# A two-layer transformer kernel: quads of the first attention turned one ahead, other orders in both output projections, a held weight split, and a helper for the second weight tile

## What is computed

```python
h = rmsnorm(x, attn_pre_g); proj = h @ w_in          # queries, keys, values, gates
o_nsa = nsa_attention(...)   # compressed, selected and window keys, 8 heads in 2 groups
o_swa = swa_attention(...)   # window of 128 keys with sinks, 8 heads in 2 groups
x = x + rmsnorm(concat(o_nsa, o_swa) @ w_o, attn_post_g)
a, u = split(rmsnorm(x, mlp_pre_g) @ w_gate_up); a = causal_dwconv(a)
x = x + rmsnorm((gelu(a) * u) @ w_down, mlp_post_g)
x = x + (p @ w_ple) * sigmoid(x @ w_ple_gate)
# second block: layer 0 differential attention (8 heads, 768 keys), layer 1 grouped queries
h = rms_norm(x, pre_g) * (1 + scale) + shift          # the same for the context
x = x + gate * rms_norm(attention(h @ w_in) @ w_out, post_g)
```

## Time and profile before

| | us |
|---|---|
| median of 3 runs (lowest, highest) | 1668.63 (1667.78, 1669.62) |
| the profiled execution, its own time | 1671.54 |
| its span, first to last instruction | 1670.2 |
| TensorE matmuls busy | 1563.2 |
| VectorE busy | 1059.8 |
| GpSimd busy | 719.2 |
| ScalarE busy | 612.8 |
| mean granted clock of TensorE | 0.976 |

### The profile page before, as it was taken

The page is one execution under the profiler, slowest core; times in us unless marked ns, Lnnn a source line. Parts: engine busy times, 40 slices in busy tenths (PEclk is TensorE's granted clock), DMA queues, the critical chain, the costliest instruction groups (busy, mean ns, idle before and its releaser), DMA issues. The chain is left out here.

```text
span 1670.2 us, 21955 instructions
## 1 busy us (share of the span) xinstructions
PE 1563.2 (94%) x7933; PEld 1294.0 (77%) x7933; DVE 1059.8 (63%) x2146; ACT 612.8 (37%) x1496; POOL 719.2 (43%) x676
## 2 busy tenths in 40 slices
PE   5899799999999999999999999999997989899997
PEld 4786444688877787877798999899985767898886
DVE  7646666457777767748866565665666468656544
ACT  3213656242122220113443544444345255344431
POOL 6856000328678648685544124412444304423330
PEclk9998999999999999999999999999998999999999
DMA  6623000315444436553321011101111411111221
GB/s 181 187 80 91 11 1 1 127 64 150 122 139 133 120 107 215 176 189 115 120 64 39 14 50 51 46 18 39 51 51 51 151 64 51 52 50 39 64 89 51
DMA packets 115884, 142.58 MB, mean 85 GB/s; under 512 B 11048, under 2 KB 75200, under 8 KB 115776
## 3 DMA queue, kind: packets, MB, share of 16 engines
q1 hardware_dynamic: 89968, 91.77, 18.1%
q10 hardware_dynamic: 25808, 49.40, 9.1%
HBM read 132.74 MB, written 8.40 MB: 85 GB/s over the span
## 5 line engine op out<-in xcount | busy, mean ns | idle before, releaser
L470 POOL TENSOR_SCALAR w_hi<-w_raw 128x512 fp32r<-128x512 f32 x316 | 247.2, 782 | 667.4 <-PE ps L485 510.7
L472 POOL TENSOR_TENSOR w_lo<-w_raw,w_hi 128x512 fp32r<-128x512 f32 x316 | 440.3, 1393 | 26.4
L483 PE MATMUL ps<-w_hi,h_hi 128*128 128x384 f32 (+2 forms) x768 | 281.1, 366 | 4.1 <-DVE x L2596 1.8
L484 PE MATMUL ps<-w_lo,h_hi 128*128 128x384 f32 (+2 forms) x768 | 267.5, 348 | 0.0
L485 PE MATMUL ps<-w_hi,h_lo 128*128 128x384 f32 (+2 forms) x768 | 266.9, 348 | 0.0
L483 PE MATMUL ps<-h_hi,w_hi 128*128 128x512 f32 (+1 forms) x616 | 246.4, 400 | 8.0 <-POOL w_lo L472 4.2
L485 PE MATMUL ps<-h_hi,w_lo 128*128 128x512 f32 (+1 forms) x616 | 239.0, 388 | 0.0
L484 PE MATMUL ps<-h_lo,w_hi 128*128 128x512 f32 (+1 forms) x616 | 238.8, 388 | 0.0
L2541 DVE SCALAR_TENSOR_TENSOR mod_acc<-mod_piece,csil,mod_acc 128x512 f32<-128x512 f32 x140 | 158.5, 1171 | 27.0 <-DMA mod_piece<-in_ada_w 22.9
L483 PEld LDWEIGHTS ps<-w_hi,h_hi 128*128 128x128 f32 x768 | 147.0, 191 | 16.0 <-DVE x L2596 2.5
L484 PEld LDWEIGHTS ps<-w_lo,h_hi 128*128 128x128 f32 x768 | 147.2, 192 | 9.7 <-issue 0.5
(11 more groups left out here) (323 smaller groups left out, 2789.3 us busy)
## 6 DMA issues: line engine op xcount, KB each, us to landing
mod_piece<-in_ada_w ACTq DMA_DIRECT2D x96, 256.0 KB, 3.2
w_raw<-in_w_gate_up SPq DMA_DIRECT2D x88, 256.0 KB, 3.2
w_raw<-in_a_w_in SPq DMA_DIRECT2D x128, 128.0 KB, 2.3
w_raw<-in_w_down SPq DMA_DIRECT2D x22, 512.0 KB, 4.0
w_raw<-in_b_w_in SPq DMA_DIRECT2D x20, 512.0 KB, 3.6
w_raw<-in_w_out SPq DMA_DIRECT2D x16, 512.0 KB, 3.8
w_raw<-in_w_in SPq DMA_DIRECT2D x8, 512.0 KB, 4.2
w_raw<-in_w_o SPq DMA_DIRECT2D x8, 512.0 KB, 3.8
```

The costliest lines, as they stand in the source:

```text
L470: pool.tensor_scalar(hi[:, e, :], raw[:, e, :], 1.0, 0.0, ALU.mult, ALU.add).then_inc(*s["pool_step"].up())
L472: m = pool.tensor_tensor(lo[:, e, :], raw[:, e, :], hi[:, e, :], ALU.subtract)
L483: pe.matmul(out, a[0], b[0], start=start, stop=False)
L484: pe.matmul(out, a[0], b[1], start=False, stop=False)
```

## The change

1. `pool_program` no longer makes the high halves of `("kv", 1)`; ScalarE makes them, one copy of 128x1024 for each pair, ahead of its copies of the keys, and GpSimd waits for each copy before its two differences.
2. The split of `("z8", 0)` waits for the query roots (`rms` of `("q8", 0)`) in place of `roped8` of the last key row.
3. `pe_quads` keeps the value product of the last chunk of a quad back until the first turn and the scores of the next quad are issued. `act_quads` makes the exponentials one chunk later, behind that chunk's copy; `dve_quads` scales the next quad ahead of the low halves of the quad before.
4. In the first output projection VectorE scales the rows (`dve_scale_row` serves both projections); its last row is rooted and scaled ahead of the low halves of row 2.
5. In the second output projection y is squared first for every row, the store of a row goes out one row later, row t - 2 is turned after the squares of row t instead of ahead of those of t + 1, and the loads of the tables and VectorE's use of them move one row later.

```diff
+BY_SCALAR = ("kv", 1)
@@ pool_program
                 if tile == ("z8", 0):
-                    pool.wait_ge(*s["roped8"].at(("kv8", TX + 1)))
+                    pool.wait_ge(*s["rms"].at(("q8", 0)))
+            if tile == BY_SCALAR:
+                pool.wait_ge(*s["act_step"].at(("w_hi", q)))
             for e in range(2):
-                pool.tensor_scalar(hi[:, e, :], raw[:, e, :], 1.0, 0.0, ALU.mult, ALU.add).then_inc(*s["pool_step"].up())
-                pool.wait_ge(*s["pool_step"].now())
+                if tile != BY_SCALAR:
+                    pool.tensor_scalar(hi[:, e, :], raw[:, e, :], 1.0, 0.0, ALU.mult, ALU.add).then_inc(*s["pool_step"].up())
+                    pool.wait_ge(*s["pool_step"].now())
@@ act_block_one_attention
+    for q in range(0, KD, 2):
+        pair = (KD + q) // 2
+        act.wait_ge(*s[f"w_loaded{pair % 2}"].at(pair))
+        act.activation(k.place(BY_SCALAR)[0][:, q:q + 2, :], k.w_raw[:, pair % 2, :, :], ACT.Copy, scale=1.0).then_inc(*s["act_step"].up(("w_hi", q)))
@@ pe_quads
+    before = None
     for q in qs:
         ahead = slots_behind(qs, q.n)
-        for i in range(len(q.chunks) + 1):
-            if i < len(q.chunks):
-                pe_quad_turn(k, pe, qs, q, i)
+        for i in range(len(q.chunks)):
+            pe_quad_turn(k, pe, qs, q, i)
             for slot in ahead[2 * i:2 * i + 2]:
                 pe_slot_scores(k, pe, qs, slot)
-            if i > 0:
-                pe_quad_values(k, pe, qs, q, i - 1)
+            if before is not None:
+                pe_quad_values(k, pe, qs, *before)
+            before = q, i
+    pe_quad_values(k, pe, qs, *before)
@@ act_quads
-        ahead = slots_behind(qs, q.n)
-        for i in range(len(q.chunks) + 1):
-            if i < len(q.chunks):
-                act_quad_copy(k, act, qs, q, i)
+        ahead, last = slots_behind(qs, q.n), len(q.chunks) - 1
+        for i in range(last + 1):
+            act_quad_copy(k, act, qs, q, i)
+            for slot in (ahead[2 * i - 2:2 * i] if i > 0 else []):
+                act_slot_exp(k, act, qs, slot)
+            if i == last:
+                for slot in ahead[2 * i:2 * i + 2]:
+                    act_slot_exp(k, act, qs, slot)
             if i == 0 and q.n > 0 and qs[q.n - 1].kind > 0:
                 outputs(qs[q.n - 1])
-            for slot in ahead[2 * i:2 * i + 2]:
-                act_slot_exp(k, act, qs, slot)
@@ dve_quads
+        if q.n + 1 < len(qs):
+            dve_quad_scale(k, dve, qs, qs[q.n + 1])
         if q.n > 0 and qs[q.n - 1].kind > 0:
             outputs(qs[q.n - 1])
-        if q.n + 1 < len(qs):
-            dve_quad_scale(k, dve, qs, qs[q.n + 1])
@@ pe_project_out, turn_out
-        pe.wait_ge(*s["scaled"].at(("out1", t)))
+        pe.wait_ge(*s["dve_step"].at(("out1", t)))
@@ act_project_out
-    act_last_scale(k, act, "y1", TX - 1, k.x2, rows, "out1")
@@ act_add
-    if before and scaled is not None:
-        act.wait_ge(*s["rms"].at((tag, t)))
-        act_scale(k, act, rows(t - 1), x[:, t - 1, :], 2 * t + 1, (scaled, t - 1))
@@ dve_add
-    if tag == "y3" and before:
-        dve_scale_row(k, dve, t - 1)
+    if before:
+        dve_scale_row(k, dve, tag, t - 1)
@@ dve_project_out
+    dve_last(k, dve, "y1", TX - 1)
+    dve.wait_ge(*s["rms"].at(("y1", "x", TX - 1)))
+    dve_scale_row(k, dve, "y1", TX - 1)
     turn_out(TX - 2)
-    dve_last(k, dve, "y1", TX - 1)
     turn_out(TX - 1)
@@ act_out0
     for t in range(TA):
-        if t >= 3:
-            turn_out(t - 3)
-        act_add(..., y_first=t == 1)
-        if t == 2:
-            act.wait_ge(*s["x_out"].at(("7", 1)))
+        act_add(..., y_first=t > 0)
+        if 1 <= t <= TX:
+            act.wait_ge(*s["added"].at(("y3", t - 1)))
+            act.dma_start(k.x_dram[:, t - 1, :], k.x7[:, t - 1, :]).then_inc(*s["x_out"].up(("7", t - 1), 16))
+        if t >= 2:
+            turn_out(t - 2)
+        if t == 3:
+            act.wait_ge(*s["x_out"].at(("7", 2)))
             ...
-        if t < TX:
-            act.wait_ge(*s["added"].at(("y3", t)))
-            act.dma_start(k.x_dram[:, t, :], k.x7[:, t, :]).then_inc(*s["x_out"].up(("7", t), 16))
-    turn_out(TA - 3)
@@ dve_out0
-        if t == TX:
+        if t == TX + 1:
             dve_query_tables(k, dve)
-        dve_add(..., y_first=t == 1)
+        dve_add(..., y_first=t > 0)
```

More of the change, by code:

```diff
@@ L879, in pe_quads @@
         pe_slot_scores(k, pe, qs, slot)
+    before = None
     for q in qs:
         ahead = slots_behind(qs, q.n)
-        for i in range(len(q.chunks) + 1):
-            if i < len(q.chunks):
-                pe_quad_turn(k, pe, qs, q, i)
+        for i in range(len(q.chunks)):
+            pe_quad_turn(k, pe, qs, q, i)
             for slot in ahead[2 * i:2 * i + 2]:
                 pe_slot_scores(k, pe, qs, slot)
-            if i > 0:
-                pe_quad_values(k, pe, qs, q, i - 1)
-        assert 2 * (len(q.chunks) + 1) >= len(ahead)
+            if before is not None:
+                pe_quad_values(k, pe, qs, *before)
+            before = q, i
+        assert 2 * len(q.chunks) >= len(ahead)
+    pe_quad_values(k, pe, qs, *before)
 def pe_mod_sum(k, pe, layer, j, bank, c0=0):
@@ L1531, in act_squares @@
     act.activation(junk[:, :], x, ACT.Square, accum_out=k.halves[:, 0, i:i + 1]).then_inc(*k.sig["sq"].up(event))
-def act_scale(k, act, out, x, i, event):
-    act.activation(out, x, ACT.Copy, scale=k.stat[:, 1, i:i + 1]).then_inc(*k.sig["scaled"].up(event))
 def act_program(k, act):
@@ L1764, in act_project_out @@
             turn_out(t - 2)
-        act_add(k, act, "y1", t, k.x2, k.y2[:, t % 2, :], O_BANKS[t % 2], rows, ("o", t, 1), "out1")
+        act_add(k, act, "y1", t, k.x2, k.y2[:, t % 2, :], O_BANKS[t % 2], rows, ("o", t, 1))
         act.wait_ge(*s["added"].at(("y1", t)))
@@ L1769, in act_project_out, with act_add @@
     turn_out(TX - 2)
-    act_last_scale(k, act, "y1", TX - 1, k.x2, rows, "out1")
     turn_out(TX - 1)
-def act_add(k, act, tag, t, x, yt, banks, rows, prod, scaled, y_first=False):
+def act_add(k, act, tag, t, x, yt, banks, rows, prod, y_first=False):
     s = k.sig
@@ L1803, in act_last_squares @@
     act_squares(k, act, x[:, t, :], rows(t), 2 * t + 3, (tag, "x", t))
-def act_last_scale(k, act, tag, t, x, rows, scaled):
-    act.wait_ge(*k.sig["rms"].at((tag, "x", t)))
-    act_scale(k, act, rows(t), x[:, t, :], 2 * t + 3, (scaled, t))
 def act_gate_up(k, act):
@@ L2138, in act_out0 @@
     for t in range(TA):
-        if t >= 3:
-            turn_out(t - 3)
-        act_add(k, act, "y3", t, k.x7, k.y7[:, t % 2, :], OUT0_BANKS[t % 3], rows, ("out0", t, 1), None, y_first=t == 1)
-        if t == 2:
-            act.wait_ge(*s["x_out"].at(("7", 1)))
+        act_add(k, act, "y3", t, k.x7, k.y7[:, t % 2, :], OUT0_BANKS[t % 3], rows, ("out0", t, 1), y_first=t > 0)
+        if 1 <= t <= TX:
[5 more added lines that the diff above has]
+            act.wait_ge(*s["x_out"].at(("7", 2)))
             act.dma_start(k.cosb[:, :, :], k.ins["cos_b"]).then_inc(*s["tabb_in"].up("all", 16))
@@ L2265, in act_out1 @@
     for t in range(TX):
-        act_add(k, act, "y4", t, k.x9, k.y9[:, t % 2, :], OUT1_BANKS[t], None, ("out1", t, 1), None)
+        act_add(k, act, "y4", t, k.x9, k.y9[:, t % 2, :], OUT1_BANKS[t], None, ("out1", t, 1))
         act.wait_ge(*s["added"].at(("y4", t)))
@@ L2569, in dve_end_copy, with dve_scale_row @@
     dve.tensor_copy(k.end_place(n), k.ps[0:KD, MOD_END_BANKS[n], 0:P]).then_inc(*s["end_copied"].up(n))
-def dve_scale_row(k, dve, t):
-    dve.tensor_scalar(k.rows6[:, t % 2, :], k.x7[:, t, :], k.stat[:, 1, 2 * t + 3:2 * t + 4], None, ALU.mult).then_inc(*k.sig["dve_step"].up(("out3", t)))
+def dve_scale_row(k, dve, tag, t):
+    out, x, event = (k.rows1[:, t, :], k.x2, "out1") if tag == "y1" else (k.rows6[:, t % 2, :], k.x7, "out3")
+    dve.tensor_scalar(out, x[:, t, :], k.stat[:, 1, 2 * t + 3:2 * t + 4], None, ALU.mult).then_inc(*k.sig["dve_step"].up((event, t)))
 def dve_add(k, dve, tag, t, x, yt, banks, gain, before, loads, y_first=False):
@@ L2903, in dve_out0 @@
             turn_out(t - 3)
-        if t == TX:
+        if t == TX + 1:
             dve_query_tables(k, dve)
         dve_add(k, dve, "y3", t, k.x7, k.y7[:, t % 2, :], OUT0_BANKS[t % 3], k.post7[:, t // TX, :], t > 0,
-                (("post7_in", "all"), (f"x7_in{min(t, TX)}", "x")), y_first=t == 1)
+                (("post7_in", "all"), (f"x7_in{min(t, TX)}", "x")), y_first=t > 0)
     turn_out(TA - 3)
@@ L2910, in dve_out0 @@
     dve.wait_ge(*s["rms"].at(("y3", "x", TA - 1)))
-    dve_scale_row(k, dve, TA - 1)
+    dve_scale_row(k, dve, "y3", TA - 1)
     turn_out(TA - 2)
```

## The result

| | us |
|---|---|
| kernel after, median of 5 runs (lowest, highest) | 1646.38 (1646.0, 1651.05) |
| kernel before, the same chip, median of 5 | 1667.78 (1666.66, 1669.62) |
| ratio, with its 95% interval | 0.9874 (0.9858 to 0.9889) |
| the profiled execution after, its own time and span | 1646.0, 1644.7 |

The change makes the kernel 21.4 us faster by the medians (18.5 to 23.7 by the interval). The sum of the prediction was 24.8, and between the two profiled executions the difference is 25.5. The time is 2.6 us above the predicted one, inside the likeliest case's range of 1639 to 1649.

A forecast was written before the change was run, and what follows sets the result against it. TensorE, busy 94% of the span, bounds the kernel through its waits. Terms 2.3 + 8 + 2.2 + 8.7 + 3.6 = 24.8 us off 1671.54 give 1646.7; less 2.9 for the runs' median, 1643.8; range 1634 to 1656.

The forecast's parts named there:

- likeliest case: Whole kernel: the forecast itself holds, 1639 to 1649 us; chance 0.50.
- E: Grouped queries: holding the first z tile's split until the query roots saves 3.6 us, between 1 and 5.
- D: Second output projection: y first and stores and turns in another order save 8.7 us, between 5 and 9.5.
- A: Second weight tile: ScalarE making the high halves saves 2.3 us, between 0 and 4.
- B: First attention: issuing the next quad's turn and scores ahead saves 8 us, between -2 and 18.
- C: First output projection: scaling on VectorE, last row ahead of row 2's low halves, saves 2.2 us, between 0.5 and 3.
- pays nothing: First attention: in tiles 0 and 1 waits move from copies to scaled rows; 8 us less gained, 1652; chance 0.18.
- main step: Second output projection: TensorE's waits for ScalarE's shifted halves go, 5.3 us, plus 2.6 of slow clock.
- sub-step of 0.8 us: Second output projection: ScalarE squares row 1's y without waiting for a sum, so a matmul's 0.8 us wait goes.
- D is VectorE's: Second output projection: VectorE's sums come no sooner, so the 5.3 us wait returns; 1649; chance 0.08.
- fourth rival: C's last scaling and three of E's first four score units wait on GpSimd; 5 us back, 1649; chance 0.08.
- slower rival: Quad boundaries: mean new waits from 1.6 us upward make the change lose, about 1704 without slack; chance 0.03.

The follow-up runs named there:

- D only: Kernel before with only the second output projection's changes (y first, new order of stores, turns and table loads): 1659.57 us, ratio 0.9952.
- E only: Kernel before with only the first z tile's split held until the query roots: 1664.10 us, ratio 0.9978.
- B only: Kernel before with only the new orders of all three engines in the first attention's quads: 1666.0 us, ratio 0.9990.
- A and B: Kernel before with ScalarE's high halves of the second weight tile and the new quad orders together: 1663.33 us, ratio 0.9969.
- the two halves: Kernel before with half of D each: y squared first for every row, 1668.02 us; stores, turns and table loads reordered, 1659.71 us.
- A only: Kernel before with only ScalarE making the second weight tile's high halves: 1666.69 us, ratio 0.9992.

## Why the prediction was nearly right, point by point

With the table's means, kernels without the part less kernels with it (for E, those without D's new order too, since it moves that stretch):

| term | predicted | profiled pair | means over the kernels |
|---|---|---|---|
| A | 2.3 | 3.7 | 124.7 - 121.1 = 3.6 |
| B (old order throughout, new as in the change) | 8 | 5.0 | 153.9 - 149.0 = 4.9 |
| C | 2.2 | 2.2 | 65.6 - 63.6 = 2.0 |
| D | 8.7 | 8.4 | 87.3 - 78.2 = 9.1 |
| E's stretch | 3.6 | 4.1 | 143.5 - 139.7 = 3.8 |
| sum | 24.8 | 23.4 | 23.4 |
| untouched, and the start | 0 | 2.1 | not an effect of the change |

The parts' stretches add up to 23.4 us, the medians to 21.4 with an interval of 18.5 to 23.7; the difference lies in code that the change doesn't touch. That the sum is only 1.4 us off is in part luck: B was 3 too high, and A's stretch made up 1.3 of it, which isn't shown to be A's. The six kernels with the old order hold their quads in 152.0 to 156.4 us, the four with the change's in 148.9 to 149.0, so B's means are firmer on the one side than on the other.

*The step that was mis-sized is B's sum*, 3 us too high. Its waits were right: 1.0, 0.85 and 0.65 us walked for a group of tile 2; 1.12, 0.97 and 0.67 found (at 217.58, 225.04 and 231.90); one wait of 1.0 expected in each group of tile 3, 0.93 and 0.92 found; tile 1 predicted at 7.4 us and found at 7.7. Two things were wrong. The prediction gave TensorE's own work in the new order no price. In tiles 2 and 3 the busy time grew from 77.0 to 80.5 us, of which one value product (1.0) only moved in across the border with tile 1: 2.5 us for twelve quads, 0.2 each. And tile 0, taken at 2.5 of its 5.7 by no walk at all, gave 0.7: its 34.66 us became 32.94, but 1.0 of that is the value product that now stands in tile 1. Together with 1 us of idle time more in tiles 2 and 3 that is the account: 0.7 + 7.7 - 3.5 = 4.9, where the prediction had 2.5 + 7.4 - 2.0. The rival "pays nothing" was right for tile 0, where the waits of turns on scaled rows grew from 4.6 to 6.0 us, the first of them to 2.48 at 157.30; it was wrong for tile 1, which paid in full.

*A* came out as walked up to pair 7, 0.1 us off where it lands and where it is split: 2.2 us of waits are gone; the one that is left is 1.95 and not 3, since TensorE came for pair 7 only at 54.27. These 2.2 us are A's: the first product of pair 7 stands 33.2 to 33.7 us behind the first weight product in the six kernels without A, and 30.6 to 31.3 in the eight with it, 33.3 and 31.1 by the means. The rest of its 3.6 isn't shown to be A's. The prediction took no clock for it; in the profiled pair the four us from 57 ran at 0.50 before and 0.57 after, and two kernels without A (D only, E only) had 1.00 there and stretches as short as 123.8 and 122.3. Six executions without A spread over 3.5 us and eight with it over 2.2.

*C* is right in size and in its limit: the last turn waits for the bank of row 2. Its stage is 2.2 us shorter in the profiled pair; the turn itself stands at 355.41, 59.5 us behind the quads' end, where it was 61.2. No run has C alone, and three of the eight kernels without it (B only, A and B, D only) took 65.3 us in this stretch, so that 1.7 to 2.2 us are C's.

*D* is right in its main step, 5.3 us of waits and the slow clock behind them. The sub-step of 0.8 us named the wrong cause: that wait went not by squaring y first but by the order of the store and the turns, as the two halves show, and only 0.45 of it went. "D is VectorE's" is refuted: no sum took the place of the shifted halves.

*E* is right in its gain: root 2.4 us, one wait of 0.60, the second unit 4.3 us sooner. Its cost was taken at 0.5 and was 1.9 beside D (waits of 0.40 and 1.16 among it); that the stretch still came out at 3.8 is luck: the slow four us behind the second unit (a clock of 0.58, some 1.7 us lost), which the prediction didn't count, are gone in the changed kernel. The fourth rival was right in its mechanism at this place alone: three of VectorE's rows in the first units took 0.9 to 1.1 us more than the same rows later. In C GpSimd stood idle until 353.62, when VectorE was in its last scaling, and the scalings took 0.75. So nothing like 5 us came back. By the Trainium skill (page "SBUF — State Buffer", section "Who interferes with whom") a VectorE instruction with two inputs in SBUF, as the rotation, is held by a GpSimd instruction that reads SBUF; the rotation at 1418.21 (1.35 us, behind the start of a difference) and the same rotation in the kernel before at 1444.18 (0.42, GpSimd idle) agree. The scalings, with one input of that size, were held as well.

One slip of the prediction changes nothing: its first paragraph puts the shifted turns into the first output projection, its part D rightly into the second.

The slower rival asked for a mean new wait of 1.6 us at the boundaries; found were at most 1.12 in tiles 2 and 3, and one of 0.48 in tile 1; only tile 0 had larger ones (2.48), and it had 1.72 before.

## What to carry to other kernels

A reordering should be costed on two accounts: the waits that it moves, and the work that it makes of the same instructions; B's walk through the waits alone was right to 0.3 us in each tile that it covered and still missed 2.5 us of TensorE's own. Where an order helps in one phase and harms in another (deferral in tile 1, at once from tile 2), it can be switched by phase, and the first quad behind the switch walked by itself: that made the quads 5.7 us shorter here, though the whole time didn't show a gain clear of its scatter. And don't read a part's gain from one pair of profiles: fixed marks in the stream and several kernels that share the code gave each stage to some tenths, where the whole time moves by several us.

## What was not expected of the hardware

- The same TensorE instructions in another order took 0.2 us more a quad: a group of tile 2 is busy 18.67 us in the new order and 18.11 in the old, both at a clock of 1.00. The steps that grew are scores ahead of a value product (1.11 for 1.03), a turn behind one (0.59 for 0.53), and value products that stand alone (2.00 for 1.86 the two).
- The same untouched 955 us stretch took 952.5 to 959.1 in fourteen executions. The longest of them had the lowest granted clock, 0.982 (0.99 in the shortest); but the clock isn't all of it: with D only the stretch took 958.3 at 0.988, with 8.1 us of waits on weight splits between 500 and 900 us, where the kernel before waited 6.0 and the changed kernel 3.7. In A only, with stretches of 0.66 to 0.69 in the quads, these took 2.4 us longer than in the kernel before.
- VectorE's scaling of a 128x768 row took 1.48 and 1.69 us when it started 0.21 and 0.02 us behind a difference of GpSimd's split, and 0.62 when it started 0.06 ahead of one, which then took 1.71 us in place of 1.29. In these rows the one that started second was held; all stand in one execution, within 11 us.
